# A decoder layer on one core: a smaller selection allowance ahead of each normalisation, one index sum moved ahead of the rotation, the value weights in two loads

## What is computed

```python
proj = h @ w_in[l] + b_in[l]
dq, dk, dv, iq, ik, iw, sq, sk, sv = jnp.split(proj, offsets, axis=-1)
...
iq = apply_rope(iq.reshape(B, S, IDX_HEADS, IDX_DIM), cos, sin)
...
rel = jax.nn.relu(jnp.einsum('bthd,bsd->bths', iqb, ik).astype(jnp.float32))
score = jnp.einsum('bths,bth->bts', rel, iwb.astype(jnp.float32)) * idx_scale
score = jnp.where(causal[None], score, -jnp.inf)
_, sel = lax.top_k(score, n_sel)
```

## Time and profile before

| | |
|---|---|
| median of 3 runs (lowest, highest) | 1494.96 us (1489.4, 1495.07) |
| profiled execution: time, span of its instructions | 1495.45 us, 1493.6 us |
| mean granted TensorE clock | 0.993 |
| TensorE busy | 1451.2 us, 97% |
| VectorE, GpSimd, ScalarE busy | 1070.8, 750.3, 499.6 us |
| share of the chain that ended last: PE, DVE, POOL | 91%, 5%, 2% |

### The profile page before, as it was taken

How to read it: one execution, slowest core, us unless ns; L and a number is a source line. 1 busy time by engine, 2 the same in 40 slices (tenths; PEclk the granted TensorE clock), 3 DMA queues, 4 the chain that set the end, 5 groups by cost and what they waited for, 6 DMA issues and landing times.

```text
span 1493.6 us, 21073 instructions
## 1 busy us (share of the span) xinstructions
PE 1451.2 (97%) x7552; PEld 1238.0 (83%) x7552; DVE 1070.8 (72%) x2091; ACT 499.6 (33%) x1050; POOL 750.3 (50%) x583
## 2 busy tenths in 40 slices
PE   7999998999899999999999999999999999999997
PEld 7878788999899987888878788888888888888885
DVE  6678899888886334944339677776777777777757
ACT  3135688988776521212202212111111111111111
POOL 4340368677500033044430676766677767867612
PEclk9999999999899999999999999999999999999999
DMA  6446266666310053021111012020201111020202
GB/s 245 165 146 169 85 210 197 177 193 204 108 43 1 1 191 99 22 85 57 57 48 37 7 51 85 3 84 29 85 29 57 57 57 57 29 85 1 85 29 85
DMA packets 61478, 128.98 MB, mean 86 GB/s; under 512 B 6976, under 2 KB 34112, under 8 KB 53696
## 3 DMA queue, kind: packets, MB, share of 16 engines
q1 hardware_dynamic: 51008, 108.76, 22.2%
q10 hardware_dynamic: 10368, 18.88, 3.5%
HBM read 100.35 MB, written 27.26 MB: 85 GB/s over the span
## 4 chain that ended last, share of the span: by engine, by line
PE 91%; DVE 5%; POOL 2%; issue 1%; ACT 1%; DMA 0%; DVEq 0%; ACTq 0%; SPq 0%; POOLq 0%
PE banks L903 25%; PE banks L905 25%; PE banks L904 25%; PE banks L1112 4%; PE banks L960 3%; PE banks L961 2%; PE banks L1099 2%; PE banks L1121 2%; PE banks L1068 2%; POOL w_lo L814 1%; PE banks L1048 1%; POOL w_hi L809 1%; DVE score L1817 0%; DMA raw<-w_v_dram 0%; DVE h_buf L2197 0%
## 5 line engine op out<-in xcount | busy, mean ns | idle before, releaser
L809 POOL TENSOR_SCALAR w_hi<-raw 128x512 fp32r<-128x512 f32 x156 | 103.7, 693 | 409.5 <-PE banks L905 211.1
L2322 DVE TENSOR_TENSOR h_buf<-h_buf,banks 128x512 f32<-128x512 f32 x320 | 202.5, 678 | 13.2 <-PE banks L905 9.7
L814 POOL TENSOR_TENSOR w_lo<-raw,w_hi 128x512 fp32r<-128x512 f32 x156 | 206.9, 1359 | 0.0
L903 PE MATMUL banks<-act_hi,w_hi 128*128 128x512 f32 x512 | 199.9, 390 | 1.7 <-DVE act_lo L2176 1.7
L904 PE MATMUL banks<-act_lo,w_hi 128*128 128x512 f32 x512 | 199.9, 390 | 0.0
L905 PE MATMUL banks<-act_hi,w_lo 128*128 128x512 f32 x512 | 199.8, 390 | 0.0
L903 PE MATMUL banks<-seven_hi,hid_hi 128*128 128x512 f32 x392 | 152.6, 389 | 0.0
L904 PE MATMUL banks<-seven_lo,hid_hi 128*128 128x512 f32 x392 | 152.5, 389 | 0.0
L905 PE MATMUL banks<-seven_hi,hid_lo 128*128 128x512 f32 x392 | 152.5, 389 | 0.0
L903 PE MATMUL banks<-w_hi,act_hi 128*128 128x512 f32 x384 | 152.1, 396 | 0.0
L905 PE MATMUL banks<-w_hi,act_lo 128*128 128x512 f32 x384 | 149.8, 390 | 0.0
(11 more groups left out here) (222 smaller groups left out, 3489.0 us busy)
## 6 DMA issues: line engine op xcount, KB each, us to landing
raw<-w_down_dram SPq DMA_DIRECT2D x16, 1024.0 KB, 4.7
raw_up<-w_up_dram SPq DMA_DIRECT2D x14, 1024.0 KB, 4.8
q_tile<-qk_dram SPq DMA_DIRECT2D x176, 64.0 KB, 2.7
qk_dram<-q_hi ACTq DMA_DIRECT2D x28, 256.0 KB, 2.1
qk_dram<-roped ACTq DMA_DIRECT2D x28, 256.0 KB, 2.6
x_raw<-x_t_dram SPq DMA_DIRECT2D x8, 512.0 KB, 8.9
raw<-wk_mem_dram SPq DMA_DIRECT2D x4, 1024.0 KB, 5.1
raw<-wv_mem_dram SPq DMA_DIRECT2D x4, 1024.0 KB, 5.8
```

The costliest lines, as they stand in the source:

```text
L809: pool.tensor_scalar(w_hi[s][:, col], source[:, col], 1.0, 1.0, ALU.mult, ALU.mult)\
L814: pool.tensor_tensor(w_lo[s][:, col], source[:, col], w_hi[s][:, col].bitcast(F32), ALU.subtract).then_inc(w_ready, 1)
L903: pe.matmul(dst, lh, rh, start=(first and n == 0), stop=False)
L2322: ins = dve.tensor_tensor(out, out, ring_m[g % 6][:], ALU.add if way > 0 else ALU.subtract)
```

## The change

Three edits. The value weights come in two transfers, the first quarter under a semaphore of its own. In `rotate_and_split` the first carried sum is made ahead of `rope_second` instead of behind it; the second and third stay. And the allowance of a band step depends on its place among four: 2.5, 2.5, 2.5 and, in the step ahead of a normalisation, 0.9.

```diff
-NARROW_EARLY, BUDGET_BAND = 0.9, 2.1
+NARROW_EARLY = 0.9
+BUDGET_BAND = [2.5, 2.5, 2.5, 0.9]
...
-            sp.dma_start(raw[0][:, 0:columns_of(0)], source_of(0)).then_inc(raw_in[0], 16)
+            rest = slice(v_piece(1).start, columns_of(0))
+            sp.dma_start(raw[0][:, v_piece(0)], source_of(0)[:, v_piece(0)]).then_inc(v_first_in, 16)
+            sp.dma_start(raw[0][:, rest], source_of(0)[:, rest]).then_inc(raw_in[0], 16)
...
             round_x(0)
+            act.wait_ge(v_first_in, 16)
+            round_v_weights(0)
             act.wait_ge(raw_in[0], 16)
-            round_v_weights(0)
...
                 carried = index_carried(v + 1)
+                for n in carried[0:1]:
+                    index_sum(n)
                 rope_second(r)
                 for part in range(2):
-                    for n in carried[part:part + 1]:
+                    for n in carried[1:2] if part else ():
                         index_sum(n)
                     if r < POOL_SPLIT:
                         split_roped(r, part)
...
-                    select_for(BUDGET_BAND if n < NS else BUDGET_DSA[DSA[min(n - NS, ND - 1)][0]], True)
+                    select_for(BUDGET_BAND[n % PAIRS] if n < NS else BUDGET_DSA[DSA[min(n - NS, ND - 1)][0]], True)
```

More of the change, by code:

```diff
@@ L508, in build_layer @@
         mem_in = sem("mem_in")
+        v_first_in = sem("v_first_in")
         x_in = sems("x_in", NK)
```

## The result

The changed kernel takes 1508.18 us in the median of six runs (1507.65 to 1508.82), beside six runs of the kernel before with a median of 1492.12 us (1488.68 to 1495.07). The ratio is 1.0104, 95% interval 1.0088 to 1.0120: 15.5 us slower by the ratio (13.1 to 17.9), 16.1 from median to median. The profiled execution of the changed kernel took 1508.07 us, 12.6 more than the profiled one of before. The forecast was 1507.5.

A forecast was written before the change was run, and what follows sets the result against it. TensorE, busy 1451.2 of 1493.6 us, was taken as the bound, so time comes only from its 42 us of idleness or its clock. Parts -0.2 + 12.1 + 0.6 = +12.5 us on the 1494.96 median gave 1507.5, range 1499 to 1513.

The forecast's parts named there:

- The mechanism: Halves 9, 11, 13: VectorE idles with the rotation behind the sum; rotation begins 3.4, 2.4, 3.8 us later, delaying later sums.
- Every sign that it named: VectorE idle 2.8, 1.6, 2.5 us; second-sum waits over 2; three more slow stretches; kv_lo wait; step 39's 2.4 us unchanged.
- Part 1: Value weights in two loads, at the start: VectorE's 0.20 us idleness before splitting weights may go; -0.2 us (0 to -0.2).
- Part 2, the stalls: First carried sum ahead of rotation: TensorE loses 2.8, 1.7, 2.9, 0 us at halves 9, 11, 13, 15, plus 1.1 for additions.
- Half 15: Carried sum ahead of rotation there: the 2.7 us wait moves one score on; change 0 us (-0.9 to +0.3).
- The additions: Rotation's two additions at halves 9 and 11, now beside GpSimd: 0.3 us more for each of four, +1.1 (-0.4 to +3.9).
- The clock: Slow stretches after stalls at halves 9, 11, 13: 3 x 1.6 less 2 x 0.6, +3.6 us; half 15's stays.
- Part 3: Band-step allowance: kv_lo wait of 2.8 us in step 35 replaces the 1.95 us normalisation wait; sum +0.6 us.
- The clock holds: Rival: the stalls come but no slow stretches follow; 12.5 less 3.6, 8.9 us slower, 1503.9 us; chance 0.15.
- half absorbed: Rival: halves 9 to 13 absorb half the delay as ScalarE or VectorE catch up; +6.0 us, 1501; chance 0.17.
- Faster: Rival: three score banks cover the late rotation, decided at the fifth score; -8.4 us, 1486.6; chance 0.08.
- Worse: Rival: additions beside GpSimd at 1.76 us (+2.8) and whole slow stretches (+1.2); +16.5 us, 1511.5; chance 0.10.

The follow-up runs named there:

- Two further orders: Kernel before, half 15 only: three carried sums ahead of the rotation, 1493.54 us, ratio 1.0008; then rotation cut in two with six carried scores, 1492.19 us, ratio 0.9996.
- with three sums ahead: Kernel before, half 15 only: all three carried sums ahead of the rotation, three rectifications ahead of ScalarE's roundings; 1493.54 us, ratio 1.0008.
- the order that used it: Kernel before, half 15 only: six carried scores instead of three, rotation cut in two with sums between; 1492.19 us beside 1493.69, ratio 0.9996.
- half 9 alone: Kernel before with the first carried sum ahead of the rotation at half 9 only, load and allowance unchanged; 1498.47 us, ratio 1.0039.
- half 15 moved alone: Kernel before with the first carried sum ahead of the rotation at half 15 only; 1493.63 us, ratio 1.0009.
- the run of the sums: Kernel before with only the first carried sum ahead of the rotation at halves 9, 11, 13 and 15; 1508.21 us, ratio 1.0105.

## Why the prediction held, step by step

**The sign and the size** were right: 1507.5 forecast, 1508.18 measured, well inside 1499 to 1513. But that the median came out within 0.7 us is in part luck. The forecast added 12.5 us to a median of three runs, 1494.96, that stood high; in the later comparisons, with 13 to 27 runs of it each, the kernel before had 1492.8 to 1493.7, and against those medians the changed kernel is 14.5 to 15.4 us slower. From one profiled execution to the other it is 12.6, because the profiled one of before was among those with the slower clock: 0.993 in the mean, with 17.0 us in slow stretches (and 3.4 us near 833 us), about 8.5 us of time. The kernel before has that in some runs and less in others, and so spreads over 6.4 us; the changed kernel had 0.988 or 0.989 in all six runs and spreads over 1.2.

**The mechanism** is the one that the prediction stepped through. With the first score of half 9 as zero, the rotation's first operation began at -1.73 us before (87.17 less 88.90) and at +1.67 after (88.94 less 87.27), the 3.4 us later that it had. Every sign that it named came: the idle VectorE, the waits on second sums, the wait on kv_lo, the unchanged wait at step 39 (2.35 us) and three slow stretches at the first three halves, the last from 138.0 us on.

**Part 1**, 0.2 us at most: 0.3 at its place, and nothing measurable in the time. In the changed kernel's own profile the first matmul was 0.66 us earlier (7.51 against 8.17 us). Of that 0.37 is the first block of x, whose rounding began earlier (4.66 against 5.03 us) and which varies from execution to execution, and 0.29 is the edit's, the 0.20 us of idleness of the earlier trace rows and a little more.

**Part 2, the stalls.** Waits on sums, in us:

| half | before | after | change | forecast |
|---|---|---|---|---|
| 9 | 0.34 | 3.55 | +3.2 | 2.8, and half of 1.1 for the additions |
| 11 | 0.83 in three | 3.31 | +2.5 | 1.7, and the other half |
| 13 | none | 2.30 | +2.3 | 2.9 |
| 15 | 2.71 | 2.56 and 0.36 | +0.2 | 0 |
| others | 0.61 | 1.06 | +0.5 | 0 |
| sum | 4.5 | 13.1 | +8.7 | 8.5 |

VectorE's idleness ahead of the first sum grew by 2.73 us at half 9, 1.74 at half 11 and 2.66 at half 13 (6.69, 3.35 and 3.86 us against 3.96, 1.61 and 1.20 ahead of the rotation), where 2.8, 1.6 and 2.5 were to show it. At half 13 the loss was sized too high, and it came at the fifth score, for sum 2, not at the sixth for sum 3. (Of the waits before, 0.34, 0.28 and 2.71 us are in the earlier trace rows; the rest is from the same views.)

**Half 15** went as stepped: the wait moved one score on. The prediction gave the reason, that for VectorE the rotation and two sums end at the same time in either order. Two further orders didn't give the wait back either.

**The additions.** The term was 1.1 us (bounds -0.4 and +3.9). Of the kernel before, the first addition and the first split at half 9 had not been shown:

```profile
87.95 1.08 DVE L1763 TENSOR_TENSOR roped<-roped,rot_part 128x512 f32<-128x512 f32 x1
...
91.09 1.25 DVE L1774 TENSOR_TENSOR roped<-roped,q_hi 128x512 fp32r<-128x512 f32 x1
```

After the change they take 1.50 and 1.75 us. The second addition went from 0.78 to 0.87. At half 11 the additions took 1.03 and 0.88 where they had taken 1.03 and 0.78, and the split 1.75 instead of 1.10. The four additions became 0.6 us longer together, and the two splits, which the term had left out though they too read two SBUF tiles and stand ahead of sum 2, 1.2: 1.8 us in all. At half 13 the second addition took 1.75 us as assumed.

By the rule in the Trainium skill (SBUF — State Buffer, section "SBUF: two separate sides") a VectorE operation with two SBUF inputs and a GpSimd operation that reads SBUF block each other for a whole instruction. The traces agree, more exactly than the prediction could tell. Each line pair is a piece of GpSimd's and the addition beside it, first at half 13 of the changed kernel, then at 195.9 us of the kernel before, where the rotation's scratch lies in one of the banks that TensorE writes:

```profile
133.71 1.28 POOL L805 TENSOR_TENSOR roped<-roped,q_hi 128x512 fp32r<-128x512 f32 x1 [18.05 <-ACT q_hi L1326]
133.79 1.75 DVE L1774 TENSOR_TENSOR roped<-roped,rot_part 128x512 f32<-128x512 f32 x1
...
195.92 1.28 POOL L814 TENSOR_TENSOR w_lo<-raw,w_hi 128x512 fp32r<-128x512 f32 x1
195.96 0.69 DVE L1763 TENSOR_TENSOR roped<-roped,banks 128x512 f32<-128x512 f32 x1
```

With both inputs in SBUF the addition ended 0.55 us after GpSimd's piece; with one input in a bank it took the 0.69 us that it takes alone. In the kernel before, all 16 of these additions and splits that began beside a piece of GpSimd with both inputs in SBUF ended 0.54 or 0.55 us after it. So such an operation lasts for what is left of the piece and 0.55 us more. The growth was small because the operations of halves 9 and 11 had begun beside such pieces before the change too: the change adds only the difference.

**The clock** was the term that was mis-sized, 3.6 us forecast. Between the first score at half 9 (88.90 us before, 87.27 after) and the product that ends the rotation stage's waits (183.84, 196.75) the changed kernel lost 14.5 us. Of these 8.7 are waits and 5.9 the clock: TensorE was busy for 89.6 us there before and for 95.5 after. Two stretches lasted 6.8 us, not 3.4, and the one behind half 15, which the prediction kept, didn't come. The 6.8 us ones begin before the waits of 3.55 and 3.31 us end (93.7 against 95.26), so a part of each, 2.7 us together (93.70 to 95.26 and 114.20 to 115.34), falls on an idle engine and costs nothing. The other 14.4 us cost half of that, 7.2, in place of the 1.7 of before.

**Part 3** was +0.6 (-0.3 to +1.8). Alone it measured +2.5 (1.0 to 3.7 by the interval). The wait at step 35 was 2.58 us, where 2.8 was taken. The threshold took 0.44 us there instead of 1.28, the third that the lower bound had, but the sign kept its 1.47. Both times the threshold ended within 0.02 us of a piece of GpSimd (before it began beside one of 372.00 to 373.30, after beside one of 383.64 to 384.36); it was waiting, as the prediction took it. The 1.95 us wait went, and the one at step 39 stayed. What the term lacked is a wait on the maximum of step 39's scores, 0.22 us before, 1.40 in this run and 1.52 in the changed kernel. In the other profiles with the old allowance it was from none to 0.84 us, so about 0.6 us of the growth at least goes with the edit. VectorE's instructions there are the same, so the likely reason is that TensorE, which no longer waits at step 36, is now ahead of it, and part of the 1.95 us came back as this. Its profiled execution also had 3.4 us more of slow clock than the one of before, which can't be put down to the edit.

**What offset it.** The clock's excess in the index part (2.3 us) and a slow stretch of 10.1 instead of 6.8 us at step 39 (0.9) were given back in the profiled execution by things that the edits don't touch: TensorE's first score came 1.6 us earlier than in the profile of before, and a slow stretch of 3.4 us near 833 us, which the profile of before had, was absent. By place: the same product of TensorE started 12.9 us later at the end of the rotation stage (183.84, 196.75), 14.3 later behind the band stage (592.58, 606.85) and 12.7 later near the end (1463.43, 1476.14). So the band stage cost 1.4 us in the profiles, not 0.6, and the agreement of 12.5 with 12.6 rests on errors that cancel.

**The rivals.** "The clock holds" fell by the windows, "half absorbed" by the table above. "Faster", three banks cover the late rotation, was to be decided at the fifth score of half 9: it waits 3.55 us for sum 2. "Worse" was half right: it took the additions at their dearest, which they aren't, and the slow stretches whole, 4.8 us, where the clock cost 5.9. The medians of the comparison lie 16.1 us apart, its 16.5.

A version that beats both kernels is the kernel before with no selection work in band step 39: 0.17% (0.07 to 0.26) faster than before. It is less than the 0.5% that the prediction's chances call no change.

## What to carry to other kernels

An operation moved ahead in an in-order queue brings its own wait with it: before moving the sum to free a bank sooner, ask when its input exists, and what in the queue then stands behind that. A wait for a released bank moves on to the next bank if the releasing engine has no idle time around it, as VectorE had almost none at half 15. Idle time inside the wait is no proof that another order helps: with three sums ahead VectorE had 1.89 us of it, and the order that used it made the wait 2.25 us instead of 4.02, one tile on. And work taken from one place ahead of a deadline goes to another place ahead of another: in step 34 it fell in front of the low part of step 35, which had nothing to spare, while the step with the longest wait kept its work because of the carried credit, so list the moved instructions step by step before trusting an allowance.

## What was not expected of the hardware

- Slow stretches around or behind a wait were 3.4, 6.8 and 10.1 us long. Waits of 3.55 and 3.31 us went with 6.8 us, one of 2.35 us with one of 1.52 shortly ahead of it with 10.1, but one of 3.60 (half 9 alone) with 3.4.
- The length of a wait doesn't decide alone whether a slow stretch follows: 2.23 us was followed by none and 2.25 by 6.8, 2.56 at half 15 by none in the changed kernel and by 3.4 with half 15 moved alone, 1.92 in the run of the sums by none where 1.95 before had been followed by 3.3. Runs of one kernel differ by some us for this reason: 5.6 us between those at a mean clock of 0.997 and those at 0.993.
- A 128x512 addition or split of the rotation, on two SBUF tiles, took 0.69 us alone; begun beside a piece of GpSimd it ended 0.54 or 0.55 us after that piece, which made 0.78 to 1.78 us. With one input in a bank it took 0.69 beside GpSimd too. A 128x1 operation took 0.44 or 1.28 us for the same work, by where in a piece of GpSimd it began.
